# The opening loads in halves, a late load of the mixers' constants, an earlier first root, and gates in one group of products

## The chip, the cores and the metric

The kernel runs on one core of one Trainium2 chip. The metric is the device time of one execution in microseconds (us). Every time below comes from the timed runs or from one profiled execution of the kernel before the change.

## The reference, cut to what matters

The program is two transformer-like blocks on a sequence of 256 tokens of width 1024, in fp32. The first block has two layers. A layer is: a half-step SwiGLU feed-forward (width 2816), a mixer with three groups of heads (SSD, mLSTM, RWKV-7) that read slices of one input projection, an output projection, and a second half-step feed-forward. The second block has one layer with attention, a convolution and a convolved SwiGLU. Every feed-forward and mixer is preceded by an RMS norm. What the change touches is:

```
x = x + 0.5 * (silu(gate) * up) @ w_down,  gate, up = split(rms_norm(x) @ w_gate_up)
u = rms_norm(x) @ w_in
ssd:    dt    = softplus(u[dt columns, 16] + dt_bias);  a_cum = cumsum(dt * -exp(a_log))
mlstm:  log_i = u[i columns, 4] + gate_bias[:4]
        log_f = log_sigmoid(u[f columns, 4] + gate_bias[4:]);  bcum = cumsum(log_f)
        uses log_i - bcum, its running maximum, and exp of both
```

## The kernel before, in words

Activations lie transposed: `X` holds the 1024 features as 8 tiles of 128 partitions by 256 tokens. All weights are laid out as one list of blocks `wst`, 1 MB each (128 partitions by 2048 floats; the down-projection's have 1408), in the order in which they are used. SyncE's queue (`sync`, L2658 on) loads block i into slot i mod 3 of the buffer `ring`, and waits before block i until block i-3 has been freed. It issues one DMA after the other, so whatever stands before a block in the program also stands before it in the queue. A program starts with the input `X` in two halves, the first constants `C`, the small part of the layer's parameters `LP` (from the column `n1` on: the norms' scales and biases), blocks 0 to 2, and then, ahead of block 3, all that the mixers need much later (`C` from 256 on, `AL`, eight small loads into `K64`, the 1.8 MB of the rest of `LP`) and `SP2`, the second block's vectors.

For most products a weight block is split: ScalarE writes its rounded high part `WH` (`act_high`, L475), VectorE the rest `WL` (`dve_low`, L480), and TensorE does three fast products for each pair (`three`, L489 to L491). ScalarE splits block q after block q-3 has been used; VectorE frees the ring's slot with the low part. The opening (`act_begin`, `dve_begin`, L547 to L577) does this in halves for block 0: ScalarE waits for all of block 0 (`landed(0)`), splits columns 0 to 1023, waits for both halves of `X` (`s_x` at 32) and for `LP` (`s_v`), writes `XNH` of features 0 to 3, and then the second half of each. VectorE follows with `WL` and `XNL`. Then ScalarE squares the 8 tiles of `X` into two buffers (`SQ`), with the high parts of blocks 1 and 2 after squares 2 and 5, and GpSimd adds them up (`pool_sum`, L540, L543); square n waits for sum n-2.

The first norm's root isn't needed for the products: it multiplies their results later. TensorE forms its sums after pair j=1 of feed-forward 0 (`root_at(0)` is 1; `pe_rstd_sums`, L521, L522), VectorE takes the reciprocal root by three Newton steps on 128x2 elements (`dve_rsqrt`, L502 to L511), and TensorE spreads it over rows after pair j=2 (`pe_rows`, L527). In VectorE's program (`dve_ffn`) the root of j=1 stands behind the low part of block 4 and behind `dve_condition`, three short operations on `SP2` that ScalarE's `act_condition` interleaves with.

In a mixer several strands of work (projection, scan, rwkv, ssd, four lanes) are interleaved on each engine by a fixed list of turns (`order_of`); up to the rwkv strand's start a round of turns is two half tiles of the projection, then one step of the scan. The scan strand's step 0 on TensorE (`pe_scan`, L1118 on) forms the gates: 8 products with the 64 columns `wdf` of `LP` (the 16 SSD columns in rows 0 to 15 and the forget gates in rows 32 to 35) into `bank[6]` columns 0 to 255, and 8 products with `wig` (the input gates, rows 32 to 35) into columns 256 to 511. These are plain fp32 products, which the profile lists as two records each. VectorE forms `z` in step 1 (L1258), ScalarE `li` with its bias in the same step (L1198), and VectorE `gr = li - cum` in step 7 (L1290). TensorE's next scan work is step 9, which transposes `cum`, `sft` and `gr`, behind waits for `rows` and `li`. `dve_start` (L1064) prepares the mixer, before the first turn.

Of the kernel before, what the change touches and what calls it, by code (L numbers as in the profile page):

```python
# [9 lines left out]
ALU = mybir.AluOpType  # L10
# [278 lines left out]
def hybrid_kernel(nc, xin, wst, lp, sp2, cst, out):  # L289
    ctx = ExitStack()  # L290
    with ctx:
# [3 lines left out]
        def sem(name):  # L295
            return ctx.enter_context(nc.semaphore(name))
# [18 lines left out]
        a_pe, a_act, a_dve = ([sig(f"a_{n}{j}") for j in range(4)] for n in ("pe", "act", "dve"))  # L315
        n_pe, n_act, n_dve, n_pool = ([sig(f"n_{n}{j}") for j in range(2)] for n in ("pe", "act", "dve", "pool"))
        c_dve, m_act, m_dve = sig("c_dve"), sig("m_act"), sig("m_dve")
        s_c, s_c2, s_x, s_v, s_lp, s_sp, s_out = (sem(n) for n in ("s_c", "s_c2", "s_x", "s_v", "s_lp", "s_sp", "s_out"))
        s_slot = [sem(f"s_slot{i}") for i in range(NSLOT)]

        bank = [ctx.enter_context(nc.psum_tensor(f"bank{i}", [128, 512], F32)) for i in range(8)]
# [132 lines left out]
        def landed(i):  # L454
            return s_slot[i % NSLOT], 16 * (i // NSLOT + 1)
# [27 lines left out]
        def dve_low(e, q, free=False):  # L483
            if in_turn(q, free):
                low_part(e, q)
# [61 lines left out]
        def act_begin(e):  # L547
            for half in range(2):
                at = slice(1024 * half, 1024 * half + 1024)
                e.wait_ge(*landed(0))  # L550
                e.do.activation(WH[:, 0, at], ring[:, 0, at], ACT.Copy).then_inc(*w_act.up("high", 0, half))
                e.wait_ge(s_x, 32)
                e.wait_ge(s_v, 16)
                for n in range(4 * half, 4 * half + 4):
                    e.do.activation(XNH[:, n, 0:T], X[:, n, :], ACT.Copy, scale=lpc("n1", n)).then_inc(*in_act.up("xnh", n))
            for n in range(KT):
                if n >= 2:
                    e.wait_ge(*in_pool.on("sum", n - 2))
                e.do.activation(SQ[:, n % 2, :], X[:, n, :], ACT.Square).then_inc(*in_act.up("sq", n))
                if n in (2, 5):  # L560
                    act_high(e, n // 3 + 1)

        def dve_begin(e):
            for half in range(2):
                at = slice(1024 * half, 1024 * half + 1024)
                e.wait_ge(*w_act.on("high", 0, half))
                e.do.tensor_tensor(WL[:, 0, at], ring[:, 0, at], WH[:, 0, at].bitcast(F32), ALU.subtract).then_inc(
                    *(w_dve.up("low", 0) if half else w_dve.up("first half")))
                e.wait_ge(s_x, 32)
                e.wait_ge(s_v, 16)  # L570
                for n in range(4 * half, 4 * half + 4):
                    e.wait_ge(*in_act.on("xnh", n))
                    e.do.scalar_tensor_tensor(XNL[:, n, 0:T], X[:, n, :], lpc("n1", n), XNH[:, n, 0:T].bitcast(F32), ALU.mult,  # L573
                                           ALU.subtract).then_inc(*in_dve.up("xnl", n))
            for q in range(1, AHEAD):
                dve_low(e, q)
# [254 lines left out]
        def dve_ffn(e, f):  # L831
            gu, dn, l = ffn_names(f)
            if f == 4:
                e.wait_ge(*b_act.on("xnh2", 0))
                e.do.memset(FP[:, :, 0:2], 0.0).then_inc(*f_dve.up("pads"))
                e.wait_ge(*f_dve.last())
            for j in range(NF):
                dve_low(e, turn_of(gu, l, ("pair", j)) + AHEAD)
                if f == 0 and j == 1:
                    dve_condition(e)  # L840
                if f < 4 and j < root_at(f):
                    continue
                if f < 4 and j == root_at(f):
                    e.wait_ge(*f_pe.on("sums", f))
                    dve_rsqrt(e, f_dve, bank[6][:, 0:2], 2, 1.0 / D, EPS, 0, ("rstd", f))
                    continue
                if f < 4 and j == root_at(f) + 1:
                    for i in range(j):
                        dve_taken(e, f, i)
                        if i:  # L850
                            dve_gated(e, f, i - 1)
                if f < 4:
                    dve_taken(e, f, j)
                else:
                    dve_conv(e, j)
                if f == 3 and j == 8:
                    e.wait_ge(*m_act.on("sh1"))
                    e.do.tensor_tensor(XNL[:, :, T:T + 2], sh1.unsqueeze(2).to_broadcast([128, KT, 2]), XNH[:, :, T:T + 2].bitcast(F32), ALU.subtract).then_inc(*m_dve.up("sh1"))
                if j >= 1:
                    dve_gated(e, f, j - 1)  # L860
            dve_gated(e, f, NF - 1)
            for n in range(KT):
                for h in range(2):
                    if h == 1:
                        e.wait_ge(*f_pe.on("dn", f, n, 1))
                        xt, by = (X2[:, n, :], gt2[:, n:n + 1]) if f == 4 else (X[:, n, :], 0.5)
                        if n < KT - 1:
                            e.do.scalar_tensor_tensor(xt, bank[n][:, T:2 * T], by, xt, ALU.mult, ALU.add).then_inc(*f_dve.up())
                            e.wait_ge(*f_dve.last())
                        e.do.scalar_tensor_tensor(xt, bank[n][:, 0:T], by, xt, ALU.mult, ALU.add).then_inc(*f_dve.up("add", f, n))  # L870
                        if f < 4:
                            e.wait_ge(*f_act.on("xnh", f, n))
                            e.do.scalar_tensor_tensor(XNL[:, n, 0:T], X[:, n, :], next_scale(f, n), XNH[:, n, 0:T].bitcast(F32),
                                                   ALU.mult, ALU.subtract).then_inc(*f_dve.up("xnl", f, n))
                    q = turn_of(dn, l, ("rows", n, h)) + AHEAD
                    dve_low(e, q)
                if n == 0 and f < 4:
                    dve_ada(e, f)
# [184 lines left out]

        def dve_start(e, l):  # L1064
            e.wait_ge(*landed_lp(l))
            e.do.memset(XM[:, :, 0:3], 0.0).then_inc(*p_dve.up())
            e.do.memset(UP[:, :, 0:1], 0.0).then_inc(*p_dve.up())
            for i in range(3):
                e.do.memset(RW[64:128, i * T:i * T + T], 0.0).then_inc(*p_dve.up())
            e.do.tensor_scalar(own, LP[:, LC["mu"]:LC["mu"] + 14], -1.0, 1.0, ALU.mult, ALU.add).then_inc(*p_dve.up())  # L1070
            e.do.tensor_scalar(LP[:, LC["sw"]:LC["sn"]], LP[:, LC["sw"]:LC["sn"]], 0.5, None, ALU.mult).then_inc(*p_dve.up("start", l))
            e.wait_ge(*p_dve.last())
# [45 lines left out]
        def pe_scan(e, l):  # L1118
            b = bank[6]
            e.wait_ge(*p_dve.on("normed", l, 4))  # L1120
            e.wait_ge(*f_dve.on("add", 2 * l, 6))
            for name, o in (("wdf", b[0:64, 0:T]), ("wig", b[0:64, T:2 * T])):
                for kt in range(KT):
                    at = LC[name] + kt * 64
                    m = e.do.matmul(o, LP[:, at:at + 64], XN[:, kt, :], start=kt == 0, stop=kt == KT - 1)  # L1125
            m.then_inc(*s_pe.up("gates", l))
            for _ in range(9):
                yield
            e.wait_ge(*s_dve.on("rows", l))
            e.wait_ge(*s_act.on("li", l))  # L1130
            for c in range(2):
                s = slice(c * 128, c * 128 + 128)
                for i, q in enumerate((cum, sft, gr)):
# [60 lines left out]
        def act_scan(e, l):  # L1194
            b = bank[6]
            yield
            e.wait_ge(*s_dve.on("z", l))
            e.do.activation(li, b[0:64, T:2 * T], ACT.Identity, bias=lpc("ib", 0, p64)).then_inc(*s_act.up("li", l))  # L1198
            e.do.activation(ab, z, ACT.Abs).then_inc(*s_act.up())
            e.wait_ge(*s_act.last())  # L1200
            e.do.activation(ex, ab, ACT.Exp, scale=-1.0).then_inc(*s_act.up())
# [52 lines left out]
        def dve_scan(e, l):  # L1254
# [32 lines left out]
                e.do.tensor_tensor_scan(cum[:, s], ones[0:64, :], z[:, s], 0.0, ALU.mult, ALU.add).then_inc(*s_dve.up("cum", l, c))  # L1287
            yield
            e.wait_ge(*s_dve.last())
            e.do.tensor_tensor(gr, li, cum, ALU.subtract).then_inc(*s_dve.up())  # L1290
            e.wait_ge(*s_dve.last())
            e.do.tensor_tensor_scan(ab[:, 0:128], ones[0:64, :], gr[:, 0:128], 0.0, ALU.mult, ALU.max).then_inc(*s_dve.up())
            e.wait_ge(*s_dve.last())
# [1362 lines left out]
            pool_ffn(e, 4)  # L2656

        def sync(e):  # L2658
            for n in range(2):
                e.do.dma_start(X[:, 4 * n:4 * n + 4, :], xin[:, 4 * n:4 * n + 4, :]).then_inc(s_x, 16)  # L2660
            e.do.dma_start(C[:, 0:256], cst[:, 0:256]).then_inc(s_c, 16)
            e.do.dma_start(LP[:, LC["n1"]:LN], lp[0, :, LC["n1"]:LN]).then_inc(s_v, 16)
            for i in range(len(plan)):
                if i == NSLOT:
                    e.do.dma_start(C[:, 256:CC["gs"]], cst[:, 256:CC["gs"]]).then_inc(s_c2, 16)
                    e.do.dma_start(AL[:, :], cst[:, CC["al"]:CC["al"] + 384]).then_inc(s_c2, 16)
                    for half in range(2):
# [2 lines left out]
                            blocks128 = cst[p, CC[name]:CC[name] + 128 * n].rearrange("p (n t) -> p n t", n=n)  # L2670
                            e.do.dma_start(K64[p, at:at + n, :], blocks128[:, :, 64 * half:64 * half + 64]).then_inc(s_c2, 16)
                    e.do.dma_start(LP[:, 0:LC["n1"]], lp[0, :, 0:LC["n1"]]).then_inc(s_lp, 16)
                    e.do.dma_start(SP2[:, :], sp2).then_inc(s_sp, 16)
                if i >= NSLOT:
                    e.wait_ge(*freed(i - NSLOT))
                n = 11 * 128 if plan[i][2][0] == "rows" else SLOT
# [184 lines left out]
```

## Time and profile before

| | us |
|---|---|
| timed runs, median of 3 | 1797.14 (1796.92 to 1803.63) |
| profiled execution, its own time | 1798.5 |
| its span (first to last instruction) | 1796.5 |
| TensorE busy | 1725.7 (96%) |
| VectorE busy | 1256.6 (70%) |
| ScalarE busy | 889.7 (50%) |
| GpSimd busy | 369.0 (21%) |
| TensorE's mean granted clock | 0.984 |

Busy time is a share of the whole span; the kernel's stages differ. The chain of waits follows the work that ended last back to the start. An idle engine costs time only where it stands on that chain. All times within the profile count from the span's start.

### The profile page before, as it was taken

The numbers are of one execution on the slowest core, as the hardware profiler recorded it, in microseconds if no ns is written. First come the engines' busy times: TensorE is split into PE (matmuls) and PEld (weight loads), VectorE is DVE, ScalarE is ACT, GpSimd is POOL, SyncE is SP. The second block draws the span as 40 slices with busy tenths as digits, with TensorE's granted clock in tenths as the row PEclk, the third lists the DMA queues.
The fourth block names the chain that finished last, engine by engine and source line by source line (L and its number), as shares of the span: only waits on it lengthen the run. The fifth ranks groups of instructions, "written<-read, shape, count | busy, mean of one in ns | idle before, by whom it ended". The sixth has DMA issues, their size and how long they took to land.

```text
span 1796.5 us, 35508 instructions
## 1 busy us (share of the span) xinstructions
PE 1725.7 (96%) x15248; PEld 1611.8 (90%) x15248; DVE 1256.6 (70%) x2101; ACT 889.7 (50%) x1566; POOL 369.0 (21%) x316
## 2 busy tenths in 40 slices
PE   7999999999899999999999999989999999979997
PEld 6999988887799998999998888779999888879987
DVE  5876675856667776677676576566787665789974
ACT  5664435323445654566443533344565555556652
POOL 3552000000212651156200000021265200121110
PEclk9999999999899999999999999989999999989999
DMA  8655522211146565565552221114556552335442
GB/s 301 238 222 194 213 94 94 75 46 49 49 162 258 214 233 185 212 252 211 194 215 92 94 95 34 40 48 166 222 210 234 188 192 104 118 141 181 174 151 104
DMA packets 44492, 282.86 MB, mean 157 GB/s; under 512 B 6064, under 2 KB 6704, under 8 KB 17712
## 3 DMA queue, kind: packets, MB, share of 16 engines
q1 hardware_dynamic: 44336, 280.60, 42.7%
q8 instruction: 120, 1.97, 0.4%
q14 instruction: 36, 0.29, 0.0%
HBM read 279.53 MB, written 1.05 MB: 156 GB/s over the span
## 4 chain that ended last, share of the span: by engine, by line
PE 83%; DVE 11%; ACT 3%; issue 1%; DMA 1%; POOL 0%; SPq 0%; DVEq 0%; ACTq 0%
PE bank L489 16%; PE bank L491 15%; PE bank L490 15%; PE bank L497 10%; PE bank L985 8%; PE bank L498 5%; PE bank L1581 4%; DVE WL L480 2%; ACT WH L475 2%; PE bank L1848 1%; PE bank L1125 1%; DVE XC L1054 1%; DMA ring<-wst 1%; PE bank L527 1%; PE bank L1858 0%
## 5 line engine op out<-in xcount | busy, mean ns | idle before, releaser
L489 PE MATMUL bank<-XNH,WH 128*128 128x256 f32 (+1 forms) x2176 | 620.7, 285 | 17.9 <-DVE XNL L573 12.3
L480 DVE TENSOR_TENSOR WL<-ring,WH 128x2048 fp32r<-128x2048 f32 (+1 forms) x235 | 509.4, 2170 | 162.9 <-ACT WH L475 162.7
L491 PE MATMUL bank<-XNH,WL 128*128 128x256 f32 (+1 forms) x2176 | 616.6, 283 | 0.0
L490 PE MATMUL bank<-XNL,WH 128*128 128x256 f32 (+1 forms) x2176 | 614.5, 282 | 0.0
L475 ACT ACTIVATE WH<-ring 128x2048 fp32r<-128x2048 f32 (+1 forms) x235 | 405.5, 1729 | 211.4 <-PE bank L491 133.1
L489 PEld LDWEIGHTS bank<-XNH,WH 128*128 128x128 f32 x2176 | 412.9, 190 | 23.6 <-DVE XNL L573 12.3
L490 PEld LDWEIGHTS bank<-XNL,WH 128*128 128x128 f32 x2176 | 414.3, 190 | 0.0
L491 PEld LDWEIGHTS bank<-XNH,WL 128*128 128x128 f32 x2176 | 414.1, 190 | 0.0
L497 PE MATMUL bank<-HP,WH 128*128 128x512 f32 x770 | 267.6, 392 | 0.8 <-POOL HP L882 0.7
L498 PE MATMUL bank<-HP,WL 128*128 128x256 f32 x770 | 215.5, 280 | 0.0
L985 PE MATMUL bank<-XN,ring 128*128 128x256 f32 x832 | 200.1, 389 | 0.0
L985 PEld LDWEIGHTS bank<-XN,ring 128*128 128x128 f32 x832 | 155.2, 194 | 21.2 <-issue 0.7
L497 PEld LDWEIGHTS bank<-HP,WH 128*128 128x128 f32 x770 | 144.6, 188 | 33.1 <-POOL HP L882 1.4
L882 POOL TENSOR_TENSOR HP<-HT,HP 128x256 fp32r<-128x256 f32 x110 | 124.5, 1142 | 177.0 <-ACT HP L726 177.0
L498 PEld LDWEIGHTS bank<-HP,WL 128*128 128x128 f32 x770 | 144.6, 188 | 0.0
L714 POOL TENSOR_TENSOR ring<-ring 128x512 f32<-128x512 f32 x72 | 96.2, 1337 | 212.6 <-ACT ring L706 208.8
L1373 POOL TENSOR_TENSOR XMr<-Y,XCr 128x256 fp32r<-128x256 f32 x4 | 4.6, 1162 | 534.1 <-ACT XCr L1249 534.1
L543 POOL TENSOR_TENSOR ACC<-ACC,SQ 128x256 f32<-128x256 f32 x54 | 45.2, 837 | 260.3 <-ACT SQ L773 197.4
L706 ACT ACTIVATE ring<-ring,MOD 128x256 f32<-128x256 f32 x192 | 79.4, 496 | 14.4 <-DMA ring<-wst 14.4
L816 DVE SCALAR_TENSOR_TENSOR TT<-GT,TT 128x256 f32<-128x256 f32 x88 | 58.1, 661 | 28.0 <-ACT GT L801 28.0
L773 ACT ACTIVATE SQ<-X 128x256 f32<-128x256 f32 x32 | 13.4, 418 | 100.9 <-DVE X L870 100.9
L821 DVE SCALAR_TENSOR_TENSOR HT<-TT,HT 128x256 f32<-128x256 f32 x88 | 60.9, 693 | 3.0
(476 smaller groups left out, 2612.4 us busy)
## 6 DMA issues: line engine op xcount, KB each, us to landing
ring<-wst SPq DMA_DIRECT2D x206, 1024.0 KB, 4.8
ring<-wst SPq DMA_DIRECT2D x80, 704.0 KB, 4.2
LP<-lp SPq DMA_DIRECT2D x1, 1872.0 KB, 7.1
LP<-lp SPq DMA_DIRECT2D x1, 1792.0 KB, 8.4
X<-xin SPq DMA_DIRECT2D x2, 512.0 KB, 4.7
out<-X SPq DMA_DIRECT2D x4, 256.0 KB, 2.5
C<-cst SPq DMA_DIRECT2D x1, 193.0 KB, 10.7
AL<-cst SPq DMA_DIRECT2D x1, 192.0 KB, 10.6
```

The costliest lines, as they stand in the source:

```text
L475: e.do.activation(WH[:, slot[q], 0:n], ring[:, i % NSLOT, 0:n], ACT.Copy).then_inc(*w_act.up("high", q))
L480: e.do.tensor_tensor(WL[:, slot[q], 0:n], ring[:, i % NSLOT, 0:n], WH[:, slot[q], 0:n].bitcast(F32), ALU.subtract).then_inc(*w_dve.up("low ...
L489: e.do.matmul(o, WH[:, s, cols], xh, start=first, stop=False)
L490: e.do.matmul(o, WH[:, s, cols], xl, start=False, stop=False)
L491: return e.do.matmul(o, WL[:, s, cols], xh, start=False, stop=last)
L497: e.do.matmul(b[:, :], WH[:, s, cols], x.rearrange("p s t -> p (s t)"), start=first, stop=False)
L498: return e.do.matmul(b[:, 0:T], WL[:, s, cols], x[:, 0, :], start=False, stop=last)
L706: e.do.activation(q, q, ACT.Copy, scale=MOD[:, 48 + k:49 + k]).then_inc(*f_act.up("ada", f, n))
L714: e.do.tensor_tensor(wt[:, 0:512], wt[:, 0:512], wt[:, 512 * p:512 * p + 512], ALU.add).then_inc(*f_pool.up())
L882: e.do.tensor_tensor(HL[:, j, :], HT[:, j % 3, :], HH[:, j, :].bitcast(F32), ALU.subtract).then_inc(*f_pool.up("hl", f, j))
L985: m = e.do.matmul(b[:, 0:T], wt[:, at], XN[:, kt, :], start=kt == 0, stop=kt == KT - 1)
L1581: return each(lambda p, s: e.do.matmul(b[p, at + s.start:at + s.stop], x[p, s], y[p, s], start=True, stop=True))
```

## The change

There are four edits. First, `sync` loads block 0 and `X` in alternating halves, and each half has its own semaphore; `C` and `SP2` come after block 2, and the mixers' constants after block 8 instead of after block 2. Second, ScalarE takes the high parts of blocks 1 and 2 after squares 1 and 4. Third, VectorE takes the first root ahead of the low part of block 4. Fourth, `dve_start` copies the four input-gate columns into columns 36 to 39 of `wdf`, so that 8 products give all gates in one half of the bank; ScalarE copies that half to `li`, one product with a shifted identity brings rows 36 to 39 to rows 32 to 35 in the bank's other half (scan step 3), and `gr` reads it there and adds the bias.

```diff
         def act_begin(e):
             for half in range(2):
-                e.wait_ge(*landed(0))
+                e.wait_ge(*(landed(0) if half else (s_w, 16)))
                 e.do.activation(WH[:, 0, at], ring[:, 0, at], ACT.Copy)...
-                e.wait_ge(s_x, 32)
+                e.wait_ge(s_x[half], 16)
...
-                if n in (2, 5):
+                if n in (1, 4):
                     act_high(e, n // 3 + 1)
         def dve_begin(e):
-                e.wait_ge(s_x, 32)
+                e.wait_ge(s_x[half], 16)
         def dve_ffn(e, f):
             for j in range(NF):
+                if f == 0 and j == root_at(f):
+                    e.wait_ge(*f_pe.on("sums", f))
+                    dve_rsqrt(e, f_dve, bank[6][:, 0:2], 2, 1.0 / D, EPS, 0, ("rstd", f))
                 dve_low(e, turn_of(gu, l, ("pair", j)) + AHEAD)
                 if f == 0 and j == 1:
                     dve_condition(e)
-                if f < 4 and j < root_at(f):
+                if f < 4 and j < root_at(f) or f == 0 and j == root_at(f):
                     continue
         def dve_start(e, l):
             e.wait_ge(*landed_lp(l))
+            gates, inputs = (LP[:, LC[n]:LC[n] + 512].rearrange("p (k n) -> p k n", n=64) for n in ("wdf", "wig"))
+            e.do.tensor_copy(gates[:, :, 36:40], inputs[:, :, 32:36]).then_inc(*p_dve.up())
         def pe_scan(e, l):
-            for name, o in (("wdf", b[0:64, 0:T]), ("wig", b[0:64, T:2 * T])):
-                for kt in range(KT):
-                    at = LC[name] + kt * 64
-                    m = e.do.matmul(o, LP[:, at:at + 64], XN[:, kt, :], start=kt == 0, stop=kt == KT - 1)
+            e.wait_ge(*p_dve.on("start", l))
+            for kt in range(KT):
+                at = LC["wdf"] + kt * 64
+                m = e.do.matmul(b[0:64, 0:T], LP[:, at:at + 64], XN[:, kt, :], start=kt == 0, stop=kt == KT - 1)
             m.then_inc(*s_pe.up("gates", l))
-            for _ in range(9):
+            yield
+            yield
+            yield
+            e.wait_ge(*s_act.on("li", l))
+            e.do.matmul(b[0:64, T:2 * T], ident[0:64, 4:68], li, start=True, stop=True).then_inc(*s_pe.up("li", l))
+            for _ in range(6):
                 yield
             e.wait_ge(*s_dve.on("rows", l))
-            e.wait_ge(*s_act.on("li", l))
         def act_scan(e, l):
-            e.do.activation(li, b[0:64, T:2 * T], ACT.Identity, bias=lpc("ib", 0, p64))...
+            e.do.activation(li, b[0:64, 0:T], ACT.Copy)...
         def dve_scan(e, l):
-            e.do.tensor_tensor(gr, li, cum, ALU.subtract)...
+            e.wait_ge(*s_pe.on("li", l))
+            e.do.scalar_tensor_tensor(gr, b[0:64, T:2 * T], lpc("ib", 0, p64), cum, ALU.add, ALU.subtract)...
         def sync(e):
-            for n in range(2):
-                e.do.dma_start(X[:, 4 * n:4 * n + 4, :], xin[:, 4 * n:4 * n + 4, :]).then_inc(s_x, 16)
-            e.do.dma_start(C[:, 0:256], cst[:, 0:256]).then_inc(s_c, 16)
-            e.do.dma_start(LP[:, LC["n1"]:LN], lp[0, :, LC["n1"]:LN]).then_inc(s_v, 16)
-            for i in range(len(plan)):
+            for half in range(2):
+                at = slice(1024 * half, 1024 * half + 1024)
+                e.do.dma_start(ring[:, 0, at], wst[0, :, at]).then_inc(s_slot[0] if half else s_w, 16)
+                e.do.dma_start(X[:, 4 * half:4 * half + 4, :], xin[:, 4 * half:4 * half + 4, :]).then_inc(s_x[half], 16)
+                if half == 0:
+                    e.do.dma_start(LP[:, LC["n1"]:LN], lp[0, :, LC["n1"]:LN]).then_inc(s_v, 16)
+            for i in range(1, len(plan)):
                 if i == NSLOT:
+                    e.do.dma_start(C[:, 0:256], cst[:, 0:256]).then_inc(s_c, 16)
+                    e.do.dma_start(SP2[:, :], sp2).then_inc(s_sp, 16)
+                if i == 3 * NSLOT:
                     (C from 256, AL, eight loads of K64, LP up to n1: as before)
-                    e.do.dma_start(SP2[:, :], sp2).then_inc(s_sp, 16)
```

## Rows read from the trace of the kernel before

**Rows 1.** The page, part 4: the chain's share by engine.
```profile
PE 83%; DVE 11%; ACT 3%; issue 1%; DMA 1%; POOL 0%; SPq 0%; DVEq 0%; ACTq 0%
```
**Rows 2.** TensorE's waits, 0 to 60 us: us in total, times, longest.
```profile
PE bank L489 <- DVE XNL L573: 12.3, 1, 12.3
PE bank L527 <- DVE SM L511: 0.9, 1, 0.9
```
**Rows 3.** Timeline of SyncE's queue, 0 to 60 us: start, length, what.
```profile
0.74 0.87 SPq L2660 DMA_DIRECT2D X<-xin  x2
...
2.81 1.46 SPq L2677 DMA_DIRECT2D ring<-wst  x3
...
5.29 7.90 SPq L2671 DMA_DIRECT2D K<-cst  x8
```
**Rows 4.** DMA issues of short stretches within 0 to 14 us: last, median us to landing.
```profile
X<-xin SPq DMA_DIRECT2D x1, 512.0 KB, 4.3
X<-xin SPq DMA_DIRECT2D x1, 512.0 KB, 5.1
LP<-lp SPq DMA_DIRECT2D x1, 80.0 KB, 4.8
ring<-wst SPq DMA_DIRECT2D x3, 1024.0 KB, 8.7
LP<-lp SPq DMA_DIRECT2D x1, 1792.0 KB, 8.4
```
**Rows 5.** Timeline of ScalarE, 0 to 60 us.
```profile
9.54 1.06 ACT L551 ACTIVATE WH<-ring 128x1024 fp32r<-128x1024 f32 x1 [7.53 <-DMA ring<-wst]
10.51 1.69 ACT L555 ACTIVATE XNH<-X,LP 128x256 fp32r<-128x256 f32 x4
...
20.83 0.42 ACT L559 ACTIVATE SQ<-X 128x256 f32<-128x256 f32 x1 [2.34 <-POOL ACC L543]
...
24.52 1.92 ACT L475 ACTIVATE WH<-ring 128x2048 fp32r<-128x2048 f32 x1 [0.86 <-DMA ring<-wst]
```
**Rows 6.** Timeline of VectorE, 0 to 60 us.
```profile
11.77 1.67 DVE L573 SCALAR_TENSOR_TENSOR XNL<-X,LP,XNH 128x256 fp32r<-128x256 f32 x4
...
14.49 2.30 DVE L573 SCALAR_TENSOR_TENSOR XNL<-X,LP,XNH 128x256 fp32r<-128x256 f32 x4
...
28.95 2.29 DVE L480 TENSOR_TENSOR WL<-ring,WH 128x2048 fp32r<-128x2048 f32 x1 [0.18 <-ACT WH L475]
```
**Rows 7.** Busy time by stretch: stretch, length, each engine's busy us, granted clock, DMA.
```profile
12.31:17.75 5.44, 5.44 (x24) 5.35 (x25) 4.48 (x8) 5.13 (x9) 1.98 (x3) 1.00 1.10 347
17.75:33.14 15.39, 15.39 (x129) 15.20 (x128) 10.55 (x14) 7.62 (x10) 6.97 (x8) 1.00 0.94 367
...
455.00:460.00 5.00, 5.00 (x42) 4.03 (x42) 2.86 (x15) 0.86 (x4) 0.00 (x0) 0.67 0.00 0
```
**Rows 8.** Timeline of GpSimd, 0 to 60 us.
```profile
18.26 4.29 POOL L543 TENSOR_TENSOR ACC<-ACC,SQ 128x256 f32<-128x256 f32 x3 [0.88 <-ACT SQ L559]
23.43 2.54 POOL L543 TENSOR_TENSOR ACC<-ACC,SQ 128x256 f32<-128x256 f32 x1 [0.88 <-ACT SQ L559]
```
**Rows 9.** Timeline of TensorE, 20 to 29 us.
```profile
26.40 0.28 PE L521 MATMUL bank<-C,ACC 128*128 128x1 f32 x2
...
27.21 0.37 PE L489 MATMUL bank<-XNH,WH 128*128 128x256 f32 x1
```
**Rows 10.** Timeline of TensorE, 227 to 240 us.
```profile
232.40 7.12 PE L1125 MATMUL bank<-XN,LP 128*64 128x256 f32 x32
239.45 0.39 PE L489 MATMUL bank<-XNH,WH 128*128 128x256 f32 x1
```
**Rows 11.** Groups of TensorE's instructions by line: busy us, mean ns of one.
```profile
L1408 PE MATMUL bank<-BIG,LP 64*128 64x256 f32 x16 | 5.6, 428 | 0.0
```
**Rows 12.** Timelines of VectorE and ScalarE, 205 to 275 us.
```profile
242.94 0.53 DVE L1258 TENSOR_SCALAR RW<-bank,LP 64x256 f32<-64x256 f32 x1
...
243.50 0.47 ACT L1198 ACTIVATE RW<-bank,LP 64x256 f32<-64x256 f32 x1 [4.51 <-DVE RW L1258]
```

More of the change, by code:

```diff
@@ L317, in hybrid_kernel @@
         c_dve, m_act, m_dve = sig("c_dve"), sig("m_act"), sig("m_dve")
-        s_c, s_c2, s_x, s_v, s_lp, s_sp, s_out = (sem(n) for n in ("s_c", "s_c2", "s_x", "s_v", "s_lp", "s_sp", "s_out"))
+        s_c, s_c2, s_v, s_lp, s_sp, s_out, s_w = (sem(n) for n in ("s_c", "s_c2", "s_v", "s_lp", "s_sp", "s_out", "s_w"))
+        s_x = [sem(f"s_x{i}") for i in range(2)]
         s_slot = [sem(f"s_slot{i}") for i in range(NSLOT)]
@@ L1197, in act_scan @@
             e.wait_ge(*s_dve.on("z", l))
-            e.do.activation(li, b[0:64, T:2 * T], ACT.Identity, bias=lpc("ib", 0, p64)).then_inc(*s_act.up("li", l))
+            e.do.activation(li, b[0:64, 0:T], ACT.Copy).then_inc(*s_act.up("li", l))
             e.do.activation(ab, z, ACT.Abs).then_inc(*s_act.up())
@@ L1289, in dve_scan @@
             e.wait_ge(*s_dve.last())
-            e.do.tensor_tensor(gr, li, cum, ALU.subtract).then_inc(*s_dve.up())
+            e.wait_ge(*s_pe.on("li", l))
+            e.do.scalar_tensor_tensor(gr, b[0:64, T:2 * T], lpc("ib", 0, p64), cum, ALU.add, ALU.subtract).then_inc(*s_dve.up())
             e.wait_ge(*s_dve.last())
```

## The prediction

> **What bounds the kernel now.** I first read the chain of waits: 83% of it is TensorE's own work, 11% VectorE's [rows 1]. So TensorE's time is worth its full price wherever TensorE is busy, and a shorter wait elsewhere is worth nothing. Then TensorE's waits. In the first 60 us there are two: 12.3 us until the first `XNL`, and 0.9 us for the root [rows 2]. The list of waits shows nothing more until 205 us; between 205 and 330 us it has two, of 0.9 and 1.1 us, neither in the stretch from 232 to 275 us where the gates lie. So three things are touched: the opening, the first root, and the gates of two layers.
>
> **The opening before.** The queue issues `X` at 0.74 and 1.15, block 0 at 2.81, and is held by the eight `K64` loads until 13.2 us [rows 3]. The halves of `X` land after 4.3 and 5.1 us (5.04 and 6.3), `LP` issued at 2.12 after 4.8 (6.9); the median of blocks 0 to 2 is 8.7, and ScalarE is released by block 0 at 9.54 [rows 4, 5]. From 6.9 to 9.5 us only block 0 was to come: 1.05 MB in 2.6 us, 0.40 MB/us, my price of bandwidth below.
>
> **The opening after.** Half 0 of block 0 takes the first place in the queue and has X's size and row length, so it lands at 5.04; X's half 0 takes the second place, 6.3; `LP`, some 0.5 us earlier in the queue and with 128 KB less ahead, about 6.6. Block 0's half 1 is 0.52 MB later, 7.9; X's half 1 9.2; block 1 11.7; block 2 14.3. ScalarE: `WH` half 0 from 5.1 to 6.1, `XNH` 0 to 3 from 6.65 (after `LP`) to 8.3, `WH` half 1 to 9.3, `XNH` 4 to 7 to 10.9, by the durations of rows 5. VectorE had its first `XNL` 1.26 us after ScalarE's first `XNH` began, and TensorE started 0.54 us after that [rows 2, 5, 6]. The same distances give 7.9 and a start at 8.45 if `WL` half 0 stood in the way as before; it doesn't, since it can begin at 6.15 and ends at 7.4. The first `XNL` then starts at 7.3 and TensorE at 7.85: 4.45 us earlier than 12.3.
>
> What is late next is feature 4: ScalarE's second half, VectorE's `WL` half 1 (9.3 to 10.5), `XNL` 4, so about 11.15, where before it was 14.49 + 0.54 = 15.03 [rows 6]. That is 3.9 us earlier. TensorE is through features 0 to 3 at 10.4 and waits some 0.7 us, which it hardly did before.
>
> TensorE ran slowly at first: 24 products between 12.31 and 17.75, one per 0.227 us, then 129 in 15.39 us, one per 0.119 [rows 7]. The granted clock in these rows says 1.00 for both, but the pace halves and doubles, so the first stretch was at the lower level (1.2 GHz). If the slow stretch again lasts 5.44 us from the start it ends at 13.3; the new wait lies in it, so only 22 products fall in it instead of 24. Pair 0 (48 products) ends near 16.4, before near 20.65: 4.2 us gained. The Trainium skill ("TensorE: Matmul & The Clock Gate", Part 1) says that the monitor's window runs freely, so that the moment of the rise depends on where the first product falls in it; one trace can't show that, and it is a rival below.
>
> Block 1 must be split by 16.4. It lands at 11.7, ScalarE is free at 11.65 after squares 0 and 1 (0.71), the high part ends at 13.65 and the low part (2.29) at 16.0. No wait, by 0.4 us.
>
> Then the squares. GpSimd's sum takes 0.8 us alone, but three sums took 4.29 us and one 2.54 us, each beside a 2.29 us low part [rows 8]: it stands still while VectorE has one. That held the last sum until 25.97; TensorE took it up at 26.40, without a wait by 0.4 us, and spent 0.81 us on the sums [rows 9]. After: square 4 at 16.65 (sum 2 held by block 1's low part), high of block 2 17.0 to 18.9, low to 21.25, sum 5 at 21.85, square 7, sum 6 at 22.65. TensorE is at the sums at 16.4 + 5.7 = 22.1. So a new wait of 0.55 us (bounds 0 and 1.5). This takes the squares 1 and 4 into account: they let block 2's split begin a square sooner, block 1's too.
>
> The root: before, the low part of block 4 ended at 31.24, then came `dve_condition` and the root, until TensorE went on at 34.06, 0.92 us late. After, block 3 isn't held behind `LP` any more (before ScalarE waited for it at 24.52 [rows 5]); its low part ends near 26.5, the root (2.1 us) at 28.6. TensorE ends pair 2 at 22.65 + 0.81 + 5.93 = 29.4 and doesn't wait. The low part of block 4 ends at 31, needed at 36. So the wait of 0.92 goes, with 0.8 us to spare. Together: 34.06 − 29.4 = 4.65 us (4.2 + 0.92 − 0.55, and rounding). Bounds: 2.5 if block 1 and the sums are each a microsecond later than worked out, 6 if neither the wait at feature 4 nor that at the sums is seen.
>
> A second weighing. The Trainium skill ("DMA: Bandwidth & Descriptors", Anatomy of one DMA) gives a DMA about 2.0 us plus its bytes at 436 GB/s. By that the first half megabyte would land after 3.2 us; the trace shows 4.3 [rows 4]. The sum by the page would start TensorE about 1 us sooner. The sum here goes by the row.
>
> **The mixers' constants at block 9.** Nothing before the mixers (205 us) reads them. Their issue still holds the queue: up to 7.9 us for `K64` and some 1.5 us for the rest. Block 8 is issued when the low part of block 5 is done, near 34; so block 9 is issued at 41 to 43.5 and lands 5 to 9.8 us later (9.8 is what block 3 took behind the same `LP` load, whose own was 8.4 [rows 4]), 46 to 53. Pair 8 starts on TensorE at 30.1 + 5 × 5.7 + 0.4 = 59, so the load must land by 59 − 2.3 − 1.9 = 54.8. It is hidden, with 2 to 8 us of cover. I price it at nothing.
>
> **The gates.** 32 records from 232.40 to 239.45 [rows 10]: 7.05 us, 0.220 each, for 16 products. Eight fewer save 3.53 us. The shift product adds two records of 256 columns: by spacing as here 0.44 us; the group nearest in shape (64 partitions in) is 0.35 to 0.43 a record, so 0.86 at the worst [rows 11]; and a change between plain and fast products costs about 0.1 us each way (the first fast record after the gates took until 0.22 instead of 0.12 us later). I take 0.6. Net 2.9 us a layer, bounds 2.4 and 3.1.
>
> The new wait is TensorE's for `li`. Behind it in its queue stands the whole projection. Steps 0 to 3 have three times two half tiles between them, 6 × 1.43 = 8.6 us. Before, `z` began at 242.94 and `li` ended at 243.97, 4.5 us after the gates [rows 12]. TensorE comes 8.6 us after them: 4 us of cover. `z` itself waited behind VectorE's tile 8, which also ends 3.5 us earlier. VectorE's `gr` in step 7 waits for a product of TensorE's step 3, long past. The copy of 128 x 32 elements in `dve_start` is under 0.2 us, and TensorE didn't wait for VectorE's root there; nothing. After 290 us VectorE carries part of the chain, but its chain starts from a projection tile, so it shifts as a whole. Two layers: 5.8 us, bounds 4.8 and 6.2; a loss of more is in the rivals.
>
> **Sum.** 4.65 + 5.8 = 10.4 us. The profiled execution took 1798.5, 1.4 above the median of the runs (1797.14): 1788.1 against its own time, 1786.8 against the median. That is the forecast. A measurement of this kernel tells 0.5%, 9.0 us, from no change: the line is at 1788.1.
>
> **The rivals.**
> Late opening (0.10): block 1 or the squares' chain holds TensorE, since GpSimd's sums wait for the low parts [rows 8]. For it: covers of 0.4 us and less than nothing. Against: `LP`'s 1.8 MB is out of the way. The opening gives 2.2 instead of 4.65: 1789.2.
>
> Another phase of the clock (0.14): everything moves 4 to 10 us against the chip's own time. The slow stretch at the start may be up to 3 us longer or shorter, at half a microsecond each; and after TensorE's wait of 5.7 us near 450 us, and the same in layer 1, the granted clock was low (0.67 in 455 to 460 [rows 7]), which may shift too. Half of it on either side: about 1785 or 1788.8. For it: such stretches exist. Against: their sum in the span is only 0.016 of the clock.
>
> The gates' saving is hidden (0.07): VectorE or the exchange for `li` sets the mixers' pace, one layer or both give nothing: 1789.7 to 1792.6. For it: VectorE's 11% of the chain. Against: no wait from 232 to 275 us.
>
> The late constants (0.09) and the other side: block 9, and block 10 behind it, land after 54.8, and every microsecond beyond that is TensorE's, since ScalarE's queue stands on the load and the tanh, the low parts and block 11 are behind it. A landing at 58 gives 1790; from 65 us on the kernel is slower than before, 1799 at 67. For it: `K64` took 7.9 us to issue, and 8 small loads may be slower among full blocks. Against: block 3 behind the same loads took 9.8.
>
> That the root's wait stays, since the sums come late, is inside the first rival: 0.9.
>
> **Numbers.** Forecast 0.60, its own range 1784.5 to 1788.8, of which 0.07 lies above the line. Faster: 0.53 + 0.07 (clock) + 0.02 (gates, one layer) = 0.62. Within 0.5%: 0.07 + 0.10 + 0.07 + 0.05 + 0.04 = 0.33. Slower: 0.05. The range 1783.5 to 1791.8 takes in both bounds of the opening and the gates, the clock and one lost layer.
>
> **What would show it.** TensorE's first product near 7.9 us; a gap near 10.5; no wait for the root and a small one at the sums near 22; pair 3 begun at 30; 16 gate records of 3.5 us twice, and no wait before the shift product; no wait of ScalarE for block 9 or 10 that TensorE feels. It would be wrong if block 1 lands after 12.5, if the slow stretch is much longer, or if TensorE waits between 40 and 70 us.

## The result, and the profile after

| | before | after |
|---|---|---|
| timed runs, median (17 each) | 1798.72 us (1796.82 to 1803.63) | 1793.98 us (1792.53 to 1796.07) |
| ratio after / before | | 0.9975, 95% interval 0.9967 to 0.9982 |
| span of the profiled execution | 1796.5 us | 1793.5 us |
| mean granted clock | 0.984 | 0.981 |

The changed kernel is 4.5 us faster by the ratio. The forecast was 10.4 us, and 1793.98 lies outside its range. It stood on a median of three runs, 1797.14; seventeen give 1798.72 for the kernel before, so the ratio is the better measure. Most steps came out as worked out; one that was priced at nothing cost more than the whole opening had won.

The opening first. TensorE's timeline of the changed kernel (start, length, what, the wait in brackets), from 5 to 40 us:

```profile
7.87 0.58 PE L490 MATMUL bank<-XNH,WH 128*128 128x256 f32 x1 [7.87 <-DVE XNL L574]
...
11.01 0.58 PE L490 MATMUL bank<-XNH,WH 128*128 128x256 f32 x1 [0.21 <-DVE XNL L574]
...
22.90 0.38 PE L522 MATMUL bank<-C,ACC 128*128 128x1 f32 x2 [0.66 <-POOL SM L603]
...
29.60 0.61 PE L528 MATMUL bank<-C,SM 128*128 128x128 f32 x4
```

The first product starts at 7.87 instead of 12.3 [rows 2], the second half's at 11.01, the sums wait 0.66 us (the row names GpSimd's next small instruction; what TensorE waits for is sum 6 just before it), and the root is no longer waited for. TensorE is at 29.60 where it was at 34.06: 4.46 us won.

Then ScalarE's timeline, 44 to 62 us, and TensorE's after it:

```profile
52.74 1.92 ACT L476 ACTIVATE WH<-ring 128x2048 fp32r<-128x2048 f32 x1 [5.67 <-DMA ring<-wst]
56.71 3.31 ACT L707 ACTIVATE ring<-ring,MOD 128x256 f32<-128x256 f32 x8 [2.05 <-DMA ring<-wst]
```
```profile
67.05 0.61 PE L689 MATMUL bank<-C,AD 128*128 128x1 f32 x4 [2.19 <-POOL AD L719]
...
104.56 0.61 PE L689 MATMUL bank<-C,AD 128*128 128x1 f32 x4 [0.63 <-POOL AD L719]
```

ScalarE waits 5.67 us for block 9 and 2.05 us more for block 10, one of the condition blocks (`w_ada_2`) that lie between the pairs. ScalarE scales such a block, GpSimd adds it up (L715, L719), and TensorE has its product (L689) in its queue right behind pair 8. Before:

```profile
61.34 2.67 POOL L718 TENSOR_TENSOR AD<-ring 128x256 f32<-128x256 f32 x1
69.27 0.50 PE L688 MATMUL bank<-C,AD 128*128 128x1 f32 x4
```
After:
```profile
64.34 2.65 POOL L719 TENSOR_TENSOR AD<-ring 128x256 f32<-128x256 f32 x1
```

Before, GpSimd was done with it at 64.0 and TensorE came at 69.3: 5.3 us of cover. Now TensorE comes at 64.8 and GpSimd is done at 67.0. The wait brings a second cost, in the busy time by stretch (stretch, length, busy of TensorE, loads, VectorE, ScalarE, GpSimd, clock, DMA share, GB/s):

```profile
60.00:65.00 5.00, 4.86 (x41) 4.66 (x40) 4.61 (x3) 4.60 (x7) 4.67 (x4) 1.00 0.24 95
65.00:67.00 2.00, 0.00 (x0) 0.00 (x0) 1.41 (x1) 0.46 (x1) 2.00 (x2) 1.00 0.00 0
67.00:71.00 4.00, 3.95 (x21) 3.96 (x22) 2.78 (x5) 0.83 (x2) 2.11 (x3) 0.60 0.70 256
```

After 2.2 us without work, and 0.7 us after TensorE has gone on, the granted clock falls from 1.00 to 0.50, the lower level (1.2 GHz), for 3.4 us (0.60 as the mean of these four), and 21 products stand where 33 would fit: 1.5 to 1.7 us. The queue's timeline, and the issues from 43 to 44 us (KB, us to landing), show the cause:

```profile
35.64 1.28 SPq L2681 DMA_DIRECT2D C<-cst  x1
36.96 0.43 SPq L2682 DMA_DIRECT2D AL<-cst  x1
37.44 5.16 SPq L2687 DMA_DIRECT2D K<-cst  x8
42.64 0.59 SPq L2688 DMA_DIRECT2D LP<-lp  x1
43.28 2.24 SPq L2692 DMA_DIRECT2D ring<-wst  x2
```
```profile
LP<-lp SPq DMA_DIRECT2D x1, 1792.0 KB, 7.5
ring<-wst SPq DMA_DIRECT2D x1, 1024.0 KB, 9.4
```

Block 9's slot is free at 41.2, but it is issued at 43.28, directly behind 1.8 MB of `LP`, and lands at 52.7.

The gates are the third piece. TensorE's timelines around them in layer 0, and VectorE's next root operations, which serve as marks (L502 before, L503 after; the first mark, 128x2, stands ahead of the gates, the second, 128x16, well behind):

```profile
233.53 3.67 PE L1131 MATMUL bank<-XN,LP 128*64 128x256 f32 x16
237.13 0.39 PE L490 MATMUL bank<-XNH,WH 128*128 128x256 f32 x1
...
245.88 0.64 PE L1137 MATMUL bank<-RW,C 64*64 64x256 f32 x2
246.45 0.39 PE L490 MATMUL bank<-XNH,WH 128*128 128x256 f32 x1
```
Before:
```profile
213.98 0.16 DVE L502 TENSOR_SCALAR SM<-bank 128x2 f32<-128x2 f32 x1
294.00 0.17 DVE L502 TENSOR_SCALAR SM<-bank 128x16 f32<-128x16 f32 x1
```
After:
```profile
215.20 0.16 DVE L503 TENSOR_SCALAR SM<-bank 128x2 f32<-128x2 f32 x1
292.44 0.16 DVE L503 TENSOR_SCALAR SM<-bank 128x16 f32<-128x16 f32 x1
```

The 16 records take 3.60 us where 32 took 7.05 [rows 10], and the shift product costs about 0.7 us with its changes, without a wait: `li` is done at 241.85. Between the marks: 80.02 us before, 77.24 after, 2.8 less. In layer 1 the same marks stand at 931.28 and 1009.95 before, 929.78 and 1005.76 after: 2.7 less.

So the profile's account of 3.0 us: the opening −4.5 by 29.6 us; +5.7 from there to the first mark (−4.46 becomes +1.22), of which 2.8 are the two waits, 1.7 the slow stretch, and 1.2 small pieces up to the down-projection that the rows don't name; the gates −5.5; and +1.2 in the rest, most of it after 1580 us, where the same three waits (4.5, 2.2 and 2.2 us) are followed by a longer stretch at the low level (mean clock 0.69 over 22 us of second-block work, before 0.77; TensorE is busy for 13.0 of the 22 us in both).

### The profile page after: what moved, and what is told of

Read it like the earlier page. It is cut to its first block, busy times and chain, and to the rows that moved or that the text cites. A ratio compares the mean times of both kernels' runs of the same rounds, so it can differ in the third digit from the quotient of the medians.

```text
span 1793.5 us, 35456 instructions
## 1 busy us (share of the span) xinstructions
PE 1724.3 (96%) x15220; PEld 1610.6 (90%) x15220; DVE 1256.1 (70%) x2103; ACT 889.7 (50%) x1566; POOL 369.0 (21%) x316
## 4 chain that ended last, share of the span: by engine, by line
PE 76%; DVE 12%; ACT 5%; DMA 3%; POOL 2%; issue 1%; SPq 0%; DVEq 0%; POOLq 0%; ACTq 0%
PE bank L490 14%; PE bank L492 13%; PE bank L491 13%; PE bank L498 9%; PE bank L989 8%; PE bank L499 5%; PE bank L1592 4%; DMA ring<-wst 3%; DVE WL L481 3%; ACT WH L476 2%; POOL ring L715 1%; ACT ring L707 1%; PE bank L1859 1%; DVE XC L1058 1%; POOL AD L719 1%
## 5 line engine op out<-in xcount | busy, mean ns | idle before, releaser
L490 PEld LDWEIGHTS bank<-XNH,WH 128*128 128x128 f32 x2176 | 413.5, 190 | 20.3 <-issue 10.4
L715 POOL TENSOR_TENSOR ring<-ring 128x512 f32<-128x512 f32 x72 | 96.3, 1338 | 218.6 <-ACT ring L707 214.8
L802 ACT ACTIVATE GT<-TT 128x256 f32<-128x256 f32 x88 | 35.9, 408 | 62.3 <-DVE HT L811 62.3
```

The costliest lines, as they stand in the source:

```text
L490: e.do.matmul(o, WH[:, s, cols], xh, start=first, stop=False)
L715: e.do.tensor_tensor(wt[:, 0:512], wt[:, 0:512], wt[:, 512 * p:512 * p + 512], ALU.add).then_inc(*f_pool.up())
```

## The experiments

All ratios are to runs of the kernel before on the same chip, with 95% intervals. The theory is that the late constants eat the opening. The rivals are named in each expectation.

**The gates alone.** The fourth edit on the kernel before (its diff stands in the section on the change).

> Kernel before with the gates' edit alone (8 products and the shift product in place of 16). Theory 1 (my prediction's price): TensorE saves 3.45 us of products a layer and pays 0.6 for the shift product, without a wait for li, so 5.8 us less than before: ratio 0.9968. Rival: the gates are worth only 2 to 4 us, because a chain through VectorE takes the rest; then ratio 0.998 to 0.999, and the profile shows TensorE waits in the mixers that were not there.

Measured: 1794.77 us, 0.9966 (0.9953 to 0.9979). As forecast, 6 us by the ratio (4 to 8 us). Its profiled execution shows also that the kernel before isn't steady at the root. TensorE's waits, 0 to 60 us:

```profile
PE bank L489 <- DVE XNL L573: 12.1, 1, 12.1
PE bank L527 <- DVE SM L511: 2.9, 1, 2.9
```
and what follows, by stretch:
```profile
36.00:40.00 4.00, 4.00 (x24) 4.00 (x23) 3.35 (x6) 2.94 (x9) 1.77 (x2) 0.58 0.40 139
```

The same wait that was 0.9 us in [rows 2] is 2.9 here, because block 4, behind `LP` and block 3, reached ScalarE at 28.5 instead of 27.0, and a slow stretch (0.58) follows. The first 34 us are the same program in both.

**The opening alone.** The changed kernel without the gates' edit.

> The changed kernel without the gates' edit: loads in halves, squares, root, constants ahead of block 9. Theory 1: the 4.5 us won by the third pair of the first feed-forward are lost again between 45 and 105 us to the load of block 9 and the condition block behind it, with a stretch of slow TensorE clock after the wait: the ratio is 1.000 to 1.001 (0 to +1.5 us). Rival: the opening keeps its gain and the gates gave nothing: 0.9975.

Measured: 1802.16 us, 1.0019 (1.0011 to 1.0028). The direction is the theory's, the size was missed: 3.4 us slower, not 0 to 1.5. Its profiled execution has waits for the same two condition products as the changed kernel (1.6 and 1.1 us, 2.8 together), a slow stretch from 67.4 us on, and is 1.9 us longer than the profiled one of before. The rest isn't settled. So loads in halves, squares, root and late constants together made the kernel slower. This and the gates alone add up to 2.7 us faster where both together measured 4.5; the intervals are wide enough for that.

**The constants spread.** One part of the changed kernel is altered, the place of the mixers' constants (the wait for `LP` now counts its two pieces, which the cut below leaves out):

```diff
-                if i == 3 * NSLOT:
+                if i == 9:
                     (C from 256 on, AL: as in the changed kernel)
+                for half in range(2):
+                    if i == (13, 17)[half]:
                     (K64, four small loads each)
+                if i in (21, 25):
+                    at = slice(0, 1792) if i == 21 else slice(1792, LC["n1"])
+                    e.do.dma_start(LP[:, at], lp[0, :, at]).then_inc(s_lp, 16)
```

> The changed kernel with the mixers' constants spread: C and AL ahead of block 9, four of the eight small K64 loads ahead of block 13, four ahead of 17, half of the 1.8 MB of LP ahead of block 21 and half ahead of 25. Theory 1: each piece fits into the queue's waits for GpSimd (up to 9.7 us each), so block 9 lands near 47, ScalarE does not wait for it, TensorE does not wait for the condition products and its clock stays up; about 10 us below before (1788.5, ratio 0.9943). Rival (the loop of condition blocks, load, ScalarE, GpSimd, slot free, load, has a period of its own of about 17.6 us and sets the pace whenever TensorE comes early): the waits for the condition products stay at 2 to 3 us in total and the ratio is 0.996 to 0.997.

Measured: 1789.52 us, 0.9943 (0.9931 to 0.9955). TensorE's timeline shows no wait at the condition products, the first and the last of them 4.46 us ahead of before (69.27 and 139.48 there):

```profile
64.81 0.50 PE L689 MATMUL bank<-C,AD 128*128 128x1 f32 x4
...
135.02 0.50 PE L689 MATMUL bank<-C,AD 128*128 128x1 f32 x4
```

The marks stand at 209.61 and 286.85: −4.4 and −7.15 against before, where the forecast had −4.65 and −7.55. This shows the cause: with the constants out of the way nearly all that was forecast arrives, 10.2 us by the ratio (8.1 to 12.4) and 9.1 by the medians. The rival's waits didn't come, but the loop that it names is real. GpSimd ends the sum of block 10 here at 60.4, 4.4 us ahead of TensorE; at the product of 135.02 the cover is 1.5 us:

```profile
57.76 2.67 POOL L719 TENSOR_TENSOR AD<-ring 128x256 f32<-128x256 f32 x1
...
130.90 2.60 POOL L719 TENSOR_TENSOR AD<-ring 128x256 f32<-128x256 f32 x1
```

In the kernel before the same two covers are 5.3 and 2.6 us. The cover shrinks from round to round in both.

**The constants ahead of block 3,** where they were, with all other edits.

> The changed kernel with the mixers' constants ahead of block 3, where they were. Theory 1: the start at 7.9 stays, block 3 lands at 24.4 as before, its low part ends at 28.8 and the root at 31, so TensorE waits 1.4 us for the root and is 3 us ahead of before from there; no wait for condition products; with the gates 8.8 us below before (ratio 0.9951). Rival (loop of the condition blocks): the 3 us are lost in waits for the condition products, ratio 0.9968 as the gates alone.

Measured: 1794.01 us, 0.9969 (0.9957 to 0.9981). The rival's number, but not its mechanism. TensorE doesn't wait for condition products. It waits for the root:

```profile
33.02 1.14 PE L528 MATMUL bank<-C,SM 128*128 128x128 f32 x4 [2.98 <-DVE SM L512]
```

ScalarE got block 3 at 26.7, 2.2 us later than before; 3.0 us of wait and a slow stretch from 33 us follow, and the product behind pair 5 stands at 52.23, before at 51.71. An early start is worth nothing either if the constants stand ahead of block 3.

**Which of the constants.** Three versions of the changed kernel: `LP` issued first of the group at block 9 (the cut below); the ten small loads at 9 and `LP` at 25; `LP` at 9 and the small loads at 13, 17 and 21.

```diff
                 if i == 3 * NSLOT:
+                    e.do.dma_start(LP[:, 0:LC["n1"]], lp[0, :, 0:LC["n1"]]).then_inc(s_lp, 16)
                     (C from 256 on, AL, K64)
-                    e.do.dma_start(LP[:, 0:LC["n1"]], lp[0, :, 0:LC["n1"]]).then_inc(s_lp, 16)
```

> The changed kernel with one line moved: ahead of block 9 the 1.8 MB of LP is issued first and the ten small loads after it, instead of last. Theory 1a (it is LP's transfer, standing wholly ahead of block 9, that made it late; the small loads' issue alone costs about 2 us): LP's bytes move while the small loads are issued, block 9 is issued at 43.3 again but lands near 48 instead of 52.7, TensorE doesn't wait for the condition products; as good as the spread kernel, ratio 0.9943. Rival 1b (it is the queue being held until 43.3): block 9 lands near 52, the ratio stays 0.9975.

> The changed kernel with the ten small loads ahead of block 9 and LP ahead of block 25. Theory 1a (LP's transfer): block 9 lands near 48, no wait for the condition products, ratio 0.9943. Rival 1b (the queue held by the small loads): the ratio stays near 0.9975.

> The changed kernel with LP alone ahead of block 9, C and AL ahead of 13, the small K64 loads ahead of 17 and 21. LP is issued near 35.7 and is through by 42, when block 9's slot has just become free (41.2). Both theories on block 9 expect no wait: ratio 0.9943; a ratio of 0.996 or more would say that 1.8 MB more in this stretch harms wherever it stands.

Measured: `LP` first 1791.90 us, 0.9957 (0.9943 to 0.9971); small loads at 9 1789.05 us, 0.9942 (0.9930 to 0.9955); `LP` alone at 9 1790.43 us, 0.9952 (0.9939 to 0.9964). With the small loads alone block 9 is issued at 42.64, almost as late as in the changed kernel, and lands after 5.1 us; ScalarE doesn't wait for it. So the held queue isn't the cause, and 1b falls. But 1a is only half right. `LP` issued first took 10.4 us to land, with 1 MB of block 8 still ahead of it (alone behind block 8 it took 9.2). Its bytes did go first: of packets under 512 B, which the `K64` loads consist of, 16 moved from 36 to 44 us and 1285 from 45 to 48. But so the small loads took 6.2 to 9.1 us to land instead of 2.2 to 5.1, and their short packets moved right ahead of block 9 and beside it, which was itself issued 1.1 us later than in the changed kernel:

```profile
35.77 1.43 SPq L2681 DMA_DIRECT2D LP<-lp  x1
...
44.40 11.91 SPq L2692 DMA_DIRECT2D ring<-wst  x4
```

ScalarE waited for it until 51.7:

```profile
51.72 1.92 ACT L476 ACTIVATE WH<-ring 128x2048 fp32r<-128x2048 f32 x1 [4.52 <-DMA ring<-wst]
54.15 3.31 ACT L707 ACTIVATE ring<-ring,MOD 128x256 f32<-128x256 f32 x8 [0.52 <-DMA ring<-wst]
```

In its waits TensorE pays 2.2 us for condition products, at 83.6 and 102.5, without a slow stretch. With `LP` alone ScalarE waits 3.0 us for block 10 and TensorE 0.5 us. The cost follows `LP`'s transfer; the small loads ahead of it or behind it add to it.

**The root's place.** The spread kernel with edit 3 undone (root behind the low part of block 4 and `dve_condition`).

> The spread kernel with the first root again behind the low part of block 4 and the three condition operations. My reading: the low part of block 4 ends at 28.8, the root at 31.9, TensorE would take it up at 29.6, so it waits 2.3 us, and a stretch of slow clock of up to 1.7 us follows if the wait is long enough: ratio 0.9955 to 0.9965 against 0.9943. Rival (the early third block alone took the root's wait away, so the reordering is worth nothing): 0.9943.

Measured: 1791.87 us, 0.9959 (0.9946 to 0.9971), 2.35 us slower than the spread kernel by the medians. TensorE waits 1.8 us, and the clock is at the lower level from 32.8 us on for 3.4 us:

```profile
28.00:36.00 8.00, 6.17 (x41) 5.97 (x40) 5.97 (x19) 5.58 (x11) 0.97 (x1) 0.80 0.76 276
```

The two kernels were run on different chips, each against its own runs of before, and the intervals overlap; the profile carries the verdict. The rival falls: the order is worth something.

**The constants at block 9 on the kernel before,** nothing else changed.

> The kernel before with one part of the change alone: the mixers' constants ahead of block 9 instead of block 3 (SP2 stays ahead of block 3). Theory (late constants): TensorE starts at 12.3 as before, block 3 lands some 6 us sooner so that the root's wait (0.9 us in one execution of the kernel before, 2.9 with a slow stretch in another run) goes, but block 9 is issued some 2 us later than in the changed kernel and lands near 54.5; TensorE comes to the second condition product near 68.4 instead of 64.8, so it waits under 1 us: ratio 0.9985 to 1.0000. Rival (constants at block 9 are harmless unless the opening is early): no wait for condition products at all, ratio 0.9975 to 0.9985.

Measured: 1801.25 us, 1.0011 (1.0002 to 1.0020). The theory's mechanism, but dearer than forecast (0.9985 to 1.0000): the root's wait is 0.5 us and TensorE waits 1.5 us for condition products, but these aren't at the block that I named (68.44, no wait) but at the following ones:

```profile
86.53 0.61 PE L688 MATMUL bank<-C,AD 128*128 128x1 f32 x4 [0.38 <-POOL AD L718]
...
105.47 0.61 PE L688 MATMUL bank<-C,AD 128*128 128x1 f32 x4 [1.11 <-POOL AD L718]
```

The lateness stays in the ring. GpSimd ends these blocks' sums at intervals of 18.8, 18.9 and 17.7 us, while three pairs and a condition product take TensorE 17.55. The first round is: the sum frees the slot, the next block reaches ScalarE 4.9 us later, its split takes 1.9, the next condition block is awaited for another 1.7 and scaled in 3.3, and GpSimd adds it up in 6.9. In the kernel before and in the spread one these intervals are also 17.6 to 19.1 us. Each is longer than TensorE's 17.55, so the round has nothing to spare, and what is late once stays late until the down-projection. At the first mark this profile is 1.9 us behind that of the kernel before, at its end 3.1; the second part isn't settled.

**The squares' order.** The spread kernel with the high parts after squares 2 and 5 again.

> The spread kernel with the high parts of blocks 1 and 2 again after squares 2 and 5. Theory: a square of 0.4 us more ahead of block 1's split uses up its cover of about 0.3 us, and square 5 before block 2's split has to wait for GpSimd's sum 3: within 0.5 us of the spread kernel either way, ratio 0.994 to 0.9946. Rival (the order of the squares carries the sums, which TensorE waits 0.3 us for): the wait at the sums goes and the kernel is up to 0.5 us faster.

Measured: 1788.87 us, 0.9943 (0.9930 to 0.9957). No difference from the spread kernel. The wait at the sums is gone, as the rival said, and 0.7 us of wait for block 1's low part has come in its place, as the theory said. The edit is worth nothing that can be measured.

**Whole first loads.** The spread kernel with `X` in two halves, `LP`'s small part and block 0 whole.

> The spread kernel with the first loads as they were (both halves of X, LP's small part, then block 0 whole; X's halves on their own semaphores). Theory: ScalarE is released near 9.2 us, TensorE starts at 12.0 instead of 7.9, about 4 us of the gain go: ratio 0.9965. Rival (C's place and not the halves brought the early start): 0.995 or less.

Measured: 1791.02 us, 0.9960 (0.9947 to 0.9972). TensorE starts at 11.8. At the product behind pair 5 it is 2.6 us later than in the spread kernel (49.90 against 47.26), since later starts have no gap in the first pair and no wait at the sums. The halves are worth 2.6 to 3 us, not 4.

**Together.** The small loads at block 9, `LP` at 25, the squares' old order.

> The changed kernel with the ten small loads ahead of block 9, LP's 1.8 MB ahead of block 25, and the squares' order of the kernel before. Theory: no wait for the condition products, the wait of 0.3 to 0.7 us at the first sums gone at the price of up to 0.7 us for block 1's low part, so 1788.5 to 1789.5 us, ratio 0.9940 to 0.9945, not to be told from the spread kernel. Rival (the squares' new order costs): 0.993 or less.

Measured: 1788.25 us, 0.9945 (0.9931 to 0.9958). The four best versions (this, the spread one, that with the squares' old order, the small loads at 9) can't be told from each other; each beats the kernel before by 10 us and the changed kernel by 5.

## Why the prediction was wrong, by its own steps

**The opening** (forecast 4.65 us) measured 4.46 at the same point. The start at 7.85 was 7.87, feature 4 at 11.15 was 11.01, the new wait at the sums of 0.55 was 0.66, the root's wait went. The clock rose 5.2 us after the first product, 5.4 before; so the rival of another phase at the start didn't come true. The price of 0.40 MB/us took block 0 to be alone on its way, though blocks 1 and 2 were issued by 4.3 us; the landing it gave for block 1, 11.7, was near all the same (ScalarE took it at 11.97).

**The gates** (5.8 us) measured 5.5 in the marks and 6 in the runs of the edit alone. The exchange for `li` had its cover.

**The constants at block 9** is the step that failed. "It is hidden, with 2 to 8 us of cover. I price it at nothing." The landing was forecast between 46 and 53 and was 52.7. The cover was wrong. I counted it back from TensorE's pair 8, which needs the block at 59. The first to need it was not a pair but a condition block: block 10 lands behind block 9, ScalarE takes 3.3 us for it, GpSimd 6.9, and TensorE has its product behind pair 8, at 64.8. So block 10 had to be in ScalarE's hands by 54.5; it was at 56.7. I had seen that product (0.4 us each) and only its length, not the chain ahead of it. That step cost 5.7 us instead of nothing, more than the opening's whole gain. The spread kernel splits the cover's loss: with the same opening and the constants away, block 10's sum ends at 60.4, so the opening took 0.9 of the 5.3 us of cover (the chain moved up with it by 3.6 of 4.5), and the constants put 6.6 us on a chain that had 4.4 left. The difference is the wait of 2.2.

**The rival of late constants** had the place and the right queue, with a chance of 0.09 and a first threshold of 54.8 for block 9; it decided already at 52.7, since the chain through GpSimd is longer than the one I priced. It names block 10 too, but takes both only as what ScalarE has ahead of the later pairs.

**The clock** rival named a shift of the later stretches. The profile has some 1 us of it after 1580 us; with one profile of each kernel it isn't shown to be the change's doing.

The Trainium skill ("TensorE: Matmul & The Clock Gate", "HAM oscillation — how this bites in real kernels") says that gaps in TensorE's work cost a cold stretch besides themselves. Here the traces agree on that, but the gaps that the page speaks of are longer than any of these: here the waits of 1.6, 1.8, 2.2, 2.9 and 3.0 us were each followed by 3.4 us at the low level, the 1.1 us ones were not.

The second weighing of the prediction compares unlike things: the formula of the Trainium skill ("DMA: Bandwidth & Descriptors", "Anatomy of one DMA — SWDGE (gpsimd) path") is fitted on loads that GpSimd issues, and this kernel's are SyncE's. The 4.3 us of the row neither bears it out nor speaks against it.

## What to carry to other kernels

When a transfer is moved into a busy stretch, list every consumer behind it in the same queue, through each engine that hands it on, and count the cover back from where the last engine's work is needed, not from the nearest matrix product. An opening that is made faster can take its gain out of the cover of what doesn't move up with it, so the covers must be counted at the new times, and in a ring for every round (here 4.4 us in the first, 1.5 in the last). Large constants go in pieces where the queue waits anyway.

## What the runs showed of the hardware

Of the loads at block 9 none overtook another: the ten small ones (16 to 193 KB) took 2.2 to 5.1 us to land when issued ahead of the 1.8 MB load, and 6.2 to 9.1 us when issued behind it. The packets of the eight `K64` loads are short (under 512 B), and where only they moved, from 41 to 43 us of the changed kernel, it was 0.08 and 0.11 MB in a microsecond, against 0.43 for `LP` at 47 us; their issue, 0.64 us for each load, may be what limits it. GpSimd's sums of 0.8 us stood still during VectorE's 2.29 us low parts in every profile here (one sum 2.53 or 2.54 us, two 3.40 to 3.42, three 4.29 to 4.31).
